# Moving the first down product of each expert pair ahead of the preceding pair's add in a two-layer conditioned decoder trunk

## The reference, cut to what matters

```python
gates = jnp.sum(jax.nn.one_hot(expert_idx, N_EXPERTS, dtype=jnp.float32) * w[..., None], axis=1)
out = jnp.zeros_like(t)
for e in range(N_EXPERTS):
    a = jax.nn.silu(t @ w_gate[e]) * (t @ w_up[e])
    out = out + gates[:, e:e + 1] * (a @ w_down[e])
```

## Time and profile before

| what | value |
|---|---|
| median of 3 runs | 882.49 us (882.29 to 886.41) |
| the profiled execution's own time | 882.43 us |
| span of its trace | 880.7 us |
| PE busy | 836.3 us, 95% of the span |
| DVE, ACT, POOL busy | 377.1, 127.1, 90.1 us |
| mean granted clock of PE | 0.99 of full |
| read from memory | 302.49 MB, 345 GB/s over the span |

### The profile page before, as it was taken

One profiled execution on the slowest core, in us unless ns is written; L12 is line 12 of the kernel. 1 busy time (PEld: TensorE's weight loads), 2 busy tenths in 40 slices (PEclk: granted clock), 3 DMA queues, 4 the chain that ended last, 5 costly groups with the idle time before them and its releaser, 6 DMA issues.

```text
span 880.7 us, 10831 instructions
## 1 busy us (share of the span) xinstructions
PE 836.3 (95%) x3748; PEld 393.4 (45%) x3748; DVE 377.1 (43%) x927; ACT 127.1 (14%) x341; POOL 90.1 (10%) x146
## 2 busy tenths in 40 slices
PE   6899999999999999899989999999999999989984
PEld 3584676445333333233338557754533333333331
DVE  2185867458122221221159688828621222212225
ACT  1001244012100000000010114711110000010010
POOL 1000000032100011011013000215111101010000
PEclk9999999999999999999999999999999999999998
DMA  8999993492899999999999799405489999999811
GB/s 353 431 421 432 427 396 140 167 404 97 322 429 425 425 426 426 427 426 425 426 426 423 324 421 420 183 1 203 181 365 427 425 425 426 428 426 428 378 48 48
DMA packets 23408, 304.59 MB, mean 346 GB/s; under 512 B 2720, under 2 KB 3232, under 8 KB 5280
## 3 DMA queue, kind: packets, MB, share of 16 engines
q1 hardware_dynamic: 22752, 303.14, 82.5%
q10 hardware_dynamic: 576, 0.40, 0.1%
HBM read 302.49 MB, written 1.05 MB: 345 GB/s over the span
## 4 chain that ended last, share of the span: by engine, by line
PE 89%; DVE 8%; issue 1%; POOL 1%; ACT 1%; POOLq 0%; DVEq 0%; ACTq 0%
PE ps L1710 25%; PE ps L1718 13%; PE ps L1723 7%; PE ps L1526 7%; PE ps L1555 7%; PE ps L1539 6%; PE ps L1639 6%; PE ps L1430 2%; PE ps L1452 1%; PE ps L1732 1%; PE ps L1693 1%; PE ps L1797 1%; PE ps L1464 1%; PE ps L1588 1%; PE ps L1742 1%
## 5 line engine op out<-in xcount | busy, mean ns | idle before, releaser
L1710 PE MATMUL ps<-ring,hT 128*64 128x512 f32 x416 | 183.5, 594 | 1.9 <-POOL hT L631 1.9
L1711 PE MATMUL ps<-ring,hT 128*64 128x512 f32 x416 | 184.9, 595 | 0.0
L1710 PEld LDWEIGHTS ps<-ring,hT 128*64 128x64 f32 x416 | 55.9, 137 | 116.0 <-issue 116.0
L1231 DVE TENSOR_TENSOR arena<-arena,ps 128x256 f32<-128x256 f32 x32 | 13.5, 421 | 216.2 <-ACT arena L802 109.1
L414 DVE SCALAR_TENSOR_TENSOR spare<-ring,csig,spare 128x512 f32<-128x512 f32 x112 | 86.1, 769 | 3.8
L1719 PE MATMUL ps<-ring,arena 128*64 128x512 f32 x192 | 87.5, 598 | 0.0
L1718 PE MATMUL ps<-ring,arena 128*64 128x512 f32 x192 | 87.5, 598 | 0.0
L1723 PE MATMUL ps<-arena 128*128 128x512 f32 x144 | 66.5, 605 | 3.2 <-DVE arena L1240 3.2
L1526 PE MATMUL ps<-hT,ring 128*128 128x256 f32 x256 | 58.8, 394 | 1.5 <-ACT hT L680 1.5
L1240 DVE TENSOR_TENSOR arena<-ps,gbc 64x512 f32<-64x512 f32 x64 | 43.9, 686 | 29.6 <-PE ps L1719 28.6
L630 POOL COPY hT<-arena 128x512 f32 x32 | 19.7, 615 | 355.4 <-PE ps L1711 210.4
(11 more groups left out here) (280 smaller groups left out, 1087.7 us busy)
## 6 DMA issues: line engine op xcount, KB each, us to landing
ring<-in_moe_w_gate_dram SPq DMA_DIRECT2D x26, 2048.0 KB, 18.8
ring<-in_moe_w_up_dram SPq DMA_DIRECT2D x26, 2048.0 KB, 16.9
ring<-in_ada_w_dram SPq DMA_DIRECT2D x24, 2048.0 KB, 14.6
ring<-in_moe_w_down_dram SPq DMA_DIRECT2D x24, 2048.0 KB, 18.1
ring<-in_fox_w_in_dram SPq DMA_DIRECT2D x6, 2048.0 KB, 20.8
spare<-in_moe_w_up_dram SPq DMA_DIRECT2D x6, 2048.0 KB, 19.0
stream<-in_moe_w_gate_dram SPq DMA_DIRECT2D x6, 2048.0 KB, 20.1
ring<-in_kv_ada_w_dram SPq DMA_DIRECT2D x4, 2048.0 KB, 15.6
```

The costliest lines, as they stand in the source:

```text
L1710: t.matmul(ps[0:CAP, bank, :], lhs(k), wcols(ng)[:, k, :], start=(k == 0), stop=(k == KC - 1))
L1711: mm = t.matmul(ps[CAP:P, bank, :], lhs(k), wcols(nu)[:, k, :], start=(k == 0), stop=(k == KC - 1))
```

## The change

The loop of PE is changed, and nothing else. `down` gets a parameter `fs` that says which of its four steps are done. The first expert's down product, with its two waits, moves from step 5 up to the start of step 3, ahead of the add. It is now cut into steps (0), (1) and (2, 3): the first two take over the releases of n0 + 2 and n0 + 3 that the first two products of the add gave, and the last releases n0 + 4 as before. The transposes of step 4 stand behind the add as before; behind them come at once the transposes of the combine weights and the second down product.

```diff
-                def down(i, j, lhs, bank):
+                def down(i, j, lhs, bank, fs=range(4)):
 
                     n = N_MOE[l] + 6 * i + 4 + j
-                    for f in range(4):
+                    for f in fs:
...
                     overflow(i, 1)
-                    add_back(0, 0, putT, y).then_inc(used[slot(n0 + 2)], 1)
-                    add_back(0, 1, putT, y).then_inc(used[slot(n0 + 3)], 1)
+                    pe.wait_ge(at_r[0], q + 1)
+                    landed(pe, n0 + 4)
+                    down(i, 0, lambda f: aT[:, 0, f * CAP:(f + 1) * CAP], 4, (0,)).then_inc(used[slot(n0 + 2)], 1)
+                    down(i, 0, lambda f: aT[:, 0, f * CAP:(f + 1) * CAP], 4, (1,)).then_inc(used[slot(n0 + 3)], 1)
+                    down(i, 0, lambda f: aT[:, 0, f * CAP:(f + 1) * CAP], 4, (2, 3)).then_inc(used[slot(n0 + 4)], 1)
+                    add_back(0, 0, putT, y)
+                    add_back(0, 1, putT, y)
                     add_back(1, 0, putT, y)
                     add_back(1, 1, putT, y).then_inc(sc_mm, 1)
                     pe.wait_ge(gu_ev[1], q + 1)
                     for f in range(4):
                         mm = t.transpose(ps[:, 5, f * P:(f + 1) * P], gu[:, 1, f * P:(f + 1) * P], ident[:, :])
                     mm.then_inc(tg_mm[1], 1)
-                    pe.wait_ge(at_r[0], q + 1)
-                    landed(pe, n0 + 4)
-                    down(i, 0, lambda f: aT[:, 0, f * CAP:(f + 1) * CAP], 4).then_inc(used[slot(n0 + 4)], 1)
                     pe.wait_ge(putted, (q + 1) * 4)
```

## The result

The changed kernel takes 895.49 us in the median (894.43 to 901.88, 4 runs), with 884.45 us for the kernel before beside it (882.29 to 886.69, 4 runs): a ratio of 1.014, 95% interval 1.0081 to 1.0198. Measured again, beside 17 runs of the kernel before with a median of 882.17 us, it took 897.31 us (894.45 to 900.40, 4 runs): 1.0184, interval 1.0153 to 1.0215. It is slower, as forecast.

A forecast was written before the change was run, and what follows sets the result against it. PE's own list was taken as the bound, at 26.07 us per pair. Down product, add, chain and start gave 1.08 us more per pair, 17.3 over 16 pairs: 882.43 + 17.3 = 899.7 us, range 896.0 to 904.0.

The forecast's parts named there:

- The prediction's sum: From the moved down product's start to the second's: 9.00 to 9.20 us against 8.02; a pair grows 0.98 to 1.18.
- The chain: Second expert's path over ACT and DVE, from its transposes' start on PE to the signal for its down product: 1.93 us.
- PE's start after the signal: Time PE needs to start the second down product after DVE's signal: 0.06 to 0.15 us, middle 0.10.
- the 3.48: Lower price in us of the moved first down product, taken from the second one as following a product of equal width.
- The rival of the loads: Loads become the bound in the experts and swallow the hole in PE's list: not slower, 882.4 us; 5%.
- The rival of the clock: The hole repeated in each pair lowers PE's clock: 1.7 us more per pair, 27 in all, 927 us; 6%.
- The small hole: PE's hole is smaller than its chain: each pair loses 0.3 us or less, up to 886.8 us; 4%.

The follow-up runs named there:

- the longer chain: The changed kernel plus one more DVE operation in the second expert's chain, between L1231 and L1233: 903.79 us, ratio 1.0235 to the kernel before.
- the version with the cover: The changed kernel with the second expert's wait and four transposes moved ahead of the whole add: 879.0 us, ratio 0.9961 to the kernel before.
- the late-release run: The changed kernel with the first down matrix's slot released by the add's third product instead of the first down product's end: 901.87 us, one execution.

## Why the prediction was right

**What bounds the kernel.** That PE's list is the path held up: the period followed the hole in every run, up with the longer chain and down with the cover. But the hole alone is not the loss. The change opened 1.16 us of idle time per pair and the period grew by 0.94; the difference came off PE's own pieces. The seam ahead of the moved piece became 0.10 us shorter (below), the first down product takes 3.53 us in place of 3.59, and the four transposes 684.10 - 683.66 = 0.44 in place of 0.53, together 0.25, of which the other pieces take back some 0.02. The prediction's sum was right not to count the hole but the stretch from piece to piece.

**The term of the sum.** The chain was put at 1.93 us, and it is 685.59 - 683.66 = 1.93. PE's start after the signal was put at 0.06 to 0.15 and was 0.05, below both, although two waits stand in a row there. The moved down product (676.59 to 680.12) took 3.53 us within its 3.48 to 3.59, the add 3.54 against 3.53. From the start of the down product to that of the second one these are 9.05 us, within the forecast's 9.00 to 9.20. One reading behind the 3.48 was wrong: the second down product does not follow a product of its own column width but the two transposes of the combine weights; it is what stands behind it that has its width.

**The term that was left out.** A pair grew by 0.94 us where 1.08 was forecast, just below the bounds of 0.98 to 1.18. The sum compared the stretch from the start of the add with the stretch from the start of the moved down product, as if both began at the same moment. They don't: before, the add started at 672.86, and the last gate step of that pair, in the timeline of before, is

```profile
672.33 0.59 PE L1710 MATMUL ps<-stream,hT 128*64 128x512 f32 x1
```

so the add started 0.53 us after it. The moved down product starts 676.59 - 676.16 = 0.43 us after it. So the seam from a product that uses half of the array's columns to one that uses all of them is 0.10 us longer here than the seam between two half-column products (that the shape is the reason is read from these starts, not tested by itself), and the change took that seam away from the front of the stretch (another one, between the down product and the add, was in the sum within the 3.53). 9.05 - 8.02 - 0.10 = 0.93, which is the measured 0.94. Over 16 pairs the slip is 17.3 - 15.0 = 2.3 us.

**The profiled time.** 882.43 + 15.0 would have been 897.4, inside the range; the profiled execution took 894.43, as it met two clock drops fewer than the profiled execution of before. So two things brought it below the forecast's 899.7: the 2.3 us of the sum and 3.0 us of clock, which is luck. The forecast's range reached 3.7 us down from its middle, and the first median fell just out of it.

**The rival of the loads** fell: in the late-release run the period did not move, and in all traces of the changed kernel no expert product waited for a load. That the stream stood at its limit meant nothing for PE while it still had a lead. How little was left shows in the version with the cover, which is 0.34 us per pair faster than before and then waits 2.04 us for a load. The prediction's "nothing that makes a load or another engine earlier can gain anything here" holds for this change and no longer for that version. **The rival of the clock** fell as well. Over a stretch that holds the hole, the trace of after has the clock at its upper level:

```profile
683.60:686.60 3.00, 1.84 (x13) 0.97 (x13) 1.82 (x5) 0.38 (x1) 0.00 (x0) 1.00 1.03 437
```

The page of the Trainium skill that this rival leant on ("TensorE: Matmul & The Clock Gate", second failure mode) may hold for other patterns; here an idle time of 1.16 us that came back every 27 us, next to six short transposes, left the clock alone in all 16 pairs of both traces of the changed kernel. **The small hole** fell with the 1.16 us.

Another sentence of the Trainium skill bears on the hole itself: "Perfetto Trace Analysis", "Identifying Performance Opportunities", reads the same gap repeating on the busiest engine as a possible sign that SBUF or PSUM is too small for the next tile. Here the repeating gap came from the order of the work alone: with the transposes ahead of the add it was gone (0.0 us of idle time), with the same tiles and banks.

## What to carry to other kernels

When PE's list is the path, a piece of work that stands between a producer's start and the wait for its result is cover, and moving it away costs the chain's length less what is left in between: read the chain from the trace, start of the producer to the end of its last step, and subtract what stands behind the producer now. Moving the producer ahead as well, so that another piece stands behind it, gives the cover back; here that alone turned a loss of 0.94 us per pair into a gain of 0.34. When the path becomes shorter, look at the lead of the loads again: here some of the gain went into a wait for one. When the start of a moved piece is taken as that of the piece it replaces, check the seam to what stands in front of it.

## What the runs showed of the hardware that was not expected

PE's clock fell for 3.4 us at a time (for 6.7 us twice in the late-release run, for 10 us once in the changed kernel with the longer chain), at a few places that change from execution to execution: three times ahead of the closing stretch in the trace of before, once in each of the two traces of the changed kernel. The drop that was priced above cost 1.5 us, so that single executions of one kernel differ by several us while the period of a pair agrees to 0.01 us. For a change of this size the period from the trace is the better measure, and the median needs more runs.

A change between matmuls of different shapes is worth about 0.1 us: 0.53 us from the last half-column product to the add against 0.43 to another half-column product, and 0.53 us for four transposes ahead of a half-column product against 0.44 ahead of other transposes. In a loop in which PE does not wait, an order with two such changes per pair (the version with the cover) in place of four (before) has a period 0.34 us below 26.07, though no work was taken away. That the seams make all of this is an inference from the starts; they were not varied one by one.
